# Stacking the position parts of latent scores, quartering the recurrence gates, and moving three products to the results' banks

## What is computed

```python
def mla_attention(c_q, c_kv, k_r, ...):          # S = 512, 8 heads, NOPE 64, ROPE 32
    q = (rms_norm(c_q, q_norm_g) @ w_uq).reshape(B, S, 8, 96)
    q_nope, q_rope = q[..., :64], apply_rope(q[..., 64:], cos, sin)
    kv = (rms_norm(c_kv, kv_norm_g) @ w_ukv).reshape(B, S, 8, 128)
    k_nope, v = kv[..., :64], kv[..., 64:]
    k_rope = apply_rope(k_r, cos, sin)           # one for all heads
    s = (einsum('bqhd,bkhd->bhqk', q_nope, k_nope) + einsum('bqhr,bkr->bhqk', q_rope, k_rope)) * scale
    return einsum('bhqk,bkhd->bqhd', softmax(s), v)

def rg_lru(x, wa, ba, wx, bx, lam):              # 16 blocks of 64 x 64, x is the convolved branch
    r  = sigmoid(einsum('bshi,hij->bshj', xb, wa) + ba)
    ig = sigmoid(einsum('bshi,hij->bshj', xb, wx) + bx)
    log_a = -8 * r * softplus(-lam)
    h = scan(exp(log_a), sqrt(-expm1(2 * log_a)) * (ig * x))
```

## Time and profile before

| | |
|---|---|
| median of three runs | 2161.89 us (2161.06 to 2163.26) |
| profiled execution, its own time | 2162.84 us |
| profiled execution, span | 2161.0 us |
| TensorE busy | 2124.9 us (98% of the span) |
| VectorE busy | 1136.9 us (53%) |
| ScalarE busy | 765.7 us (35%) |
| mean granted clock of TensorE | 0.997 |

### The profile page before, as it was taken

How to read it: one execution, slowest core, us unless ns; L and a number is a source line. 1 busy time by engine, 2 the same in 40 slices (tenths; PEclk the granted TensorE clock), 3 DMA queues, 4 the chain that set the end, 5 groups by cost and what they waited for, 6 DMA issues and landing times.

```text
span 2161.0 us, 28431 instructions
## 1 busy us (share of the span) xinstructions
PE 2124.9 (98%) x11767; PEld 1754.6 (81%) x11767; DVE 1136.9 (53%) x1535; ACT 765.7 (35%) x1224; POOL 123.6 (6%) x110
## 2 busy tenths in 40 slices
PE   8999999999999999999999999999999999999998
PEld 6888988678888887788888887787788887888887
DVE  5655557645655557654444445775653446333333
ACT  4251424532242425543222224353643234222222
POOL 0111100200011100200000003000000002000000
PEclk9999999999999999999999999999999999999999
DMA  6313222113313122113333224234022332332321
GB/s 186 99 59 116 80 59 81 40 40 109 100 47 118 60 70 70 40 59 97 97 97 97 98 98 127 79 117 136 21 78 98 98 98 88 96 98 91 100 95 65
DMA packets 158097, 189.04 MB, mean 87 GB/s; under 512 B 4194, under 2 KB 147876, under 8 KB 157860
## 3 DMA queue, kind: packets, MB, share of 16 engines
q1 hardware_dynamic: 153204, 174.41, 25.6%
q0 software_dynamic: 4608, 13.00, 1.9%
q10 hardware_dynamic: 176, 0.07, 0.0%
HBM read 182.20 MB, written 7.36 MB: 88 GB/s over the span
## 4 chain that ended last, share of the span: by engine, by line
PE 91%; DVE 5%; ACT 2%; POOL 1%; issue 1%; DMA 0%; POOLq 0%; DVEq 0%; ACTq 0%
PE PS L963 25%; PE PS L965 25%; PE PS L964 25%; PE PS L1085 5%; PE PS L1126 3%; PE PS L1097 3%; POOL X L930 1%; PE PS L971 1%; PE PS L975 1%; PE PS L972 1%; PE PS L1239 1%; PE PS L1044 0%; DVE WL L1941 0%; DVE UL L1994 0%; DVE TMP L2279 0%
## 5 line engine op out<-in xcount | busy, mean ns | idle before, releaser
L963 PE MATMUL PS<-UH,WH 128*128 128x512 f32 x1632 | 642.7, 394 | 7.5 <-DVE WL L2351 4.7
L965 PE MATMUL PS<-UH,WL 128*128 128x512 f32 x1632 | 637.0, 390 | 0.0
L964 PE MATMUL PS<-UL,WH 128*128 128x512 f32 x1632 | 636.4, 390 | 0.0
L1482 ACT ACTIVATE WH<-WS 128x2048 fp32r<-128x2048 f32 x98 | 187.9, 1918 | 618.1 <-PE PS L965 602.5
L963 PEld LDWEIGHTS PS<-UH,WH 128*128 128x128 f32 x1632 | 307.2, 188 | 75.4 <-DVE UL L1994 6.0
L965 PEld LDWEIGHTS PS<-UH,WL 128*128 128x128 f32 x1632 | 306.9, 188 | 64.7
L964 PEld LDWEIGHTS PS<-UL,WH 128*128 128x128 f32 x1632 | 307.3, 188 | 62.9 <-issue 0.7
L1941 DVE TENSOR_TENSOR WL<-WS,WH 128x2048 fp32r<-128x2048 f32 x98 | 224.4, 2290 | 229.9 <-ACT WH L1482 229.8
L2211 DVE TENSOR_TENSOR WL<-WS,WH 128x2048 fp32r<-128x2048 f32 x44 | 100.7, 2288 | 151.2 <-ACT WH L1636 151.2
L1636 ACT ACTIVATE WH<-WS 128x2048 fp32r<-128x2048 f32 x44 | 84.4, 1917 | 248.9 <-PE PS L965 246.7
L963 PE MATMUL PS<-WH,UH 128*128 128x256 f32 x416 | 118.6, 285 | 0.9 <-DVE PT L2310 0.9
(11 more groups left out here) (312 smaller groups left out, 3090.9 us busy)
## 6 DMA issues: line engine op xcount, KB each, us to landing
WS<-in_ffn_w SPq DMA_DIRECT2D x66, 1024.0 KB, 5.2
WS<-in_w_in SPq DMA_DIRECT2D x61, 1024.0 KB, 5.3
WS<-in_w_out SPq DMA_DIRECT2D x8, 1024.0 KB, 5.1
WS<-in_w_gate SPq DMA_DIRECT2D x8, 1024.0 KB, 5.5
WS<-in_w_attn_out SPq DMA_DIRECT2D x4, 1024.0 KB, 5.1
WS<-in_w_lru_out SPq DMA_DIRECT2D x4, 1024.0 KB, 5.2
WS<-in_w_o SPq DMA_DIRECT2D x4, 1024.0 KB, 5.1
bias_skewed<-bias_rows POOLq DMA_DIRECT2D x1, 3072.0 KB, 13.4
```

The source lines that it names most:

```text
L963: nc.tensor.matmul(dst, sh, mh, start=start, stop=False, skip_group_check=True)
L964: nc.tensor.matmul(dst, sh, ml, start=False, stop=False, skip_group_check=True)
L965: return nc.tensor.matmul(dst, sl, mh, start=False, stop=stop, skip_group_check=True)
L1482: nc.scalar.activation(WH[:, c % 2, 0:kt * n], staged(c, kt * n), ACT.Copy).then_inc(w_hi, 1)
```

## The change

It has eight parts.

1. *Position parts stacked.* The query tiles `QRH`, `QRL` and key tiles `KRH`, `KRL` give way to `QRS` and `KRS`, where high, high and low of a head's queries stand on 96 partitions against high, low and high of the keys. One product of 96 rows per head takes the place of three of 32. ScalarE fills two quarters of a head's stack (`stack_high`), VectorE the third (`stack_low`), heads 0 and 1 ahead of the items and heads 2 to 7 after items 0, 1, 2, 3, 6 and 7 of a layer. `QRH` now lies over `SQ`.
2. *Latent attention's start.* Scores wait for the first half of the low keys only; the second half is made after the first maxima. `expanded_values(1)` goes to pair 3. The table of the exponential is loaded ahead of the queries.
3. *Latent norms.* The second sum and the spread stand between the steps of `("ga", 1)`. All norms inside a product spread one step earlier.
4. *Products in pair 3.* `("v", 1)` of the dilated attention and `("xg", 3)` go to pair 3 as well.
5. *Gates on quarters.* A gate product becomes two of 64 x 64 weights; those of the second gate write the other half of the partitions, and ScalarE reads them across. `RGW` loses its zeros and the memset ahead of its load. Two buffers `XC`; `gated` runs one round later.
6. *Start.* `input_turned(1)` comes ahead of the first product, and the next two one round earlier; the product of the bias table moves behind the second dilated group.
7. *Order of a weight chunk.* `c0 + 3` is rounded earlier in the second layer, and later on VectorE in the first.
8. *POOL.* Its first transfers change places.

```diff
-                if (w, g, hh) == ("v", 0, 0):
+                if (w, g, hh) == ("v", 0, 0) or (w, g) == ("v", 1):
                     pl.aside((w, L, hh, g), "a", 3)
...
-                     lambda: pl.aside(("uv", L, 1), "a", 2))
+                     lambda: pl.aside(("uv", L, 1), "a", 3))
...
+    pl.aside(("xg", 3), "d", 3)
+    pl.add_chunk(("xg", 3), KD, CW, ("xg", 3))
...
-                for q, k in ((QRH, KRH), (QRH, KRL), (QRL, KRH)):
-                    for b in range(2):
-                        rows = slice((2 * j + b) % 4 * ROPE, (2 * j + b) % 4 * ROPE + ROPE)
-                        got.append((b, 0, S, q[rows, j // 2, tok], k[rows, :], False))
+                for b in range(2):
+                    got.append((b, 0, S, QRS[0:3 * ROPE, (2 * j + b) % 4, tok], KRS[0:3 * ROPE, :], False))
...
+        def heads_to_stack(name, n):
+            i = n - pl.item_at[name][0]
+            return {0: 2, 1: 3, 2: 4, 3: 5, 6: 6, 7: 7}.get(i)
...
                 if k == 5:
                     norm_sum(name, KD)
-                if k == 7:
+                if k == 6:
                     norm_spread(name)
...
                     for w in range(2):
-                        last = nc.tensor.matmul(pair(key)[:, w, :], RGW[:, w, 2 * j + m, :], XC[:, m, :],
-                                                start=True, stop=True)
+                        for b in range(2):
+                            last = nc.tensor.matmul(pair(key)[rows_of(b if w == 0 else 1 - b), w, :],
+                                                    RGW[rows_of(b), w, 2 * j + m, :], XC[rows_of(b), j % 2, m, :],
+                                                    start=True, stop=True, skip_group_check=True)
...
             input_turned(0)
             idle_products(9, bank(3)[:, 0:P])
+            input_turned(1)
...
-                    if c == 0 and k < 6:
-                        input_turned(1 + k // 2)
+                    if c == 0 and k < 4:
+                        input_turned(2 + k // 2)
...
-                norm_sum(("cq", L), QT)
-                norm_sum(("ckv", L), KT_KV)
-
-                def spread_c():
-                    norm_spread(("cq", L))
-                    norm_spread(("ckv", L))
-
-                feature_major(("ga", L, 1), between=spread_c)
+                def latent_norms(k):
+                    if k == 0:
+                        norm_sum(("cq", L), QT)
+                    if k == 1:
+                        norm_sum(("ckv", L), KT_KV)
+                    if k == 3:
+                        norm_spread(("cq", L))
+                        norm_spread(("ckv", L))
+
+                feature_major(("ga", L, 1), between=latent_norms)
...
-                pe.wait_ge(dve_out, pl.dve_out["uk", L, 1])
+                pe.wait_ge(dve_out, pl.dve_out["uk", L, 0])
                 pe.wait_ge(krope_lo, L + 1)
-                pe.wait_ge(qrope_lo, L + 1)
...
+            def stack_high(name, h):
+                if h >= 4:
+                    act.wait_ge(acc_ready, place_free(name, h))
+                for i in range(2):
+                    ins = nc.scalar.activation(QRS[quarter(i), h % 4, :],
+                                               QRH[quarter(h % 4), h // 4, :].bitcast(F32), ACT.Copy)
+                ins.then_inc(stack_hi, 1)
...
+            def stack_low(name, h):
+                if h >= 4:
+                    dve.wait_ge(acc_ready, place_free(name, h))
+                nc.vector.scalar_tensor_tensor(out=QRS[quarter(2), h % 4, :], in0=TMP[quarter(h % 4), h // 4, :],
+                                               scalar=MLA_SCALE, in1=QRH[quarter(h % 4), h // 4, :].bitcast(F32),
+                                               op0=ALU.mult, op1=ALU.subtract).then_inc(stack_lo, 1)
...
-                        if hh == 1 or i > (L == 0):
+                        if hh == 0 and i == 0:
+                            lo_of_chunk(c0 + 3)
+                        if hh == 1 or i > 1:
                             lo_of_chunk(pl.chunk[key] + 2)
...
-                if j > 0:
-                    dve.wait_ge(acc_ready, pl.acc["rg", 2 * j - 1])
-                    dve.wait_ge(gate_v, 2 * j)
+                if j > 1:
+                    dve.wait_ge(acc_ready, pl.acc["rg", 2 * j - 3])
+                    dve.wait_ge(gate_v, 2 * j - 2)
```

More of the change, by code:

```diff
@@ L441, in build_program @@
                               for i, name in enumerate(("QNH", "QNL", "KNH", "KNL")))
[L442 to L445, removed]
+        KRS = place("KRS", [P, S], F32R, offset=arena_at + 4 * 8192)
+        QRS = place("QRS", [P, 4, S], F32R, offset=arena_at + 4 * 15360)
         VM = view(6144, NT, S)
@@ L991, in feature_major @@
                         norm_between(norm, k)
-                    if between and k == 3:
-                        between()
+                    if between:
+                        between(k)
                     if new and new[0] == "cat":
@@ L1081, in scores @@
                     take_pair(("item", n))
+                    if kind == "mla" and it["first"]:
+                        pe.wait_ge(stack_hi, 8 * it["L"] + 2 * it["j"] + 2)
+                        pe.wait_ge(stack_lo, 8 * it["L"] + 2 * it["j"] + 2)
                     last = [None, None]
@@ L1283, in vectors_turned @@
                 last.then_inc(small_pe, 1)
-                pe.wait_ge(rel_in, 48)
-                nc.tensor.matmul(bank(6)[0:QH, 0:384], TBL, ONEHOT, start=True, stop=True).then_inc(small_pe, 1)
             input_turned(0)
             idle_products(9, bank(3)[:, 0:P])
+            input_turned(1)
             for k in range(0, KD, 2):
@@ L1321, in _ @@
                             continue
+                        if (w, L, hh, g) == ("k", 0, 0, 1):
+                            pe.wait_ge(small_dve, 2)
+                            pe.wait_ge(rel_in, 48)
+                            nc.tensor.matmul(bank(5)[0:QH, 0:384], TBL, ONEHOT, start=True, stop=True
+                                             ).then_inc(small_pe, 1)
                         if w == "v":
@@ L1424, in _, with last_queries @@
             pe.wait_ge(keys_in, 64)
-            attention(("swa",), lambda: feature_major(("wq", 3)))
+            def last_queries():
+                pe.wait_ge(dve_out, pl.dve_out["xg", 3])
+                feature_major(("wq", 3))
+            attention(("swa",), last_queries)
             for j in range(8):
@@ L1605, in attention @@
                 mla = name[0] == "mla"
-                table(ACT.Exp)
+                if not mla:
+                    table(ACT.Exp)
                 exp_of_item(n0)
@@ L1613, in attention @@
                     turned(n)
+                    if mla and heads_to_stack(name, n):
+                        stack_high(name, heads_to_stack(name, n))
                     if n > n0 and pl.items[n - 1]["last"] and not mla:
@@ L1759, in _ @@
                 act.wait_ge(krope_ready, L + 1)
[L1760 removed]
+                nc.scalar.activation(KRS[:, :], KRO[:, 0, :], ACT.Copy).then_inc(krope_hi, 1)
                 table(ACT.Sqrt)
@@ L1785, in _ @@
                                              ).then_inc(qrope_hi, 1)
+                        act.wait_ge(qrope_hi, L + 1)
+                        for h in range(2):
+                            stack_high(("mla", L), h)
                 def values_out(u):
@@ L2163, in attention @@
                     turned(n)
+                    if mla and heads_to_stack(name, n):
+                        stack_low(name, heads_to_stack(name, n))
                     if mla and it["last"]:
@@ L2437, in _, with low_keys @@
                 dve.wait_ge(qrope_hi, L + 1)
-                nc.vector.scalar_tensor_tensor(out=QRL[:, :, :], in0=TMP[:, :, :], scalar=MLA_SCALE,
-                                               in1=QRH[:, :, :].bitcast(F32), op0=ALU.mult, op1=ALU.subtract
-                                               ).then_inc(qrope_lo, 1)
-                for u in range(2):
+                for h in range(2):
+                    stack_low(("mla", L), h)
+                def low_keys(u):
                     key = ("uk", L, u)
@@ L2445, in _ @@
                        ).then_inc(dve_out, 1)
-                attention(("mla", L))
+                low_keys(0)
+                attention(("mla", L), lambda: low_keys(1))
                 for j in range(4):
```

90 lines of the change are left out of this document (58 added, 32 removed).

## The result

The changed kernel takes 2139.62 us (median of four runs, 2138.69 to 2140.05) against 2161.52 beside it on the same chip: ratio 0.9897, 95% interval 0.9886 to 0.9909. Forecast was 2127.0, range 2121 to 2139. The sign was right, 12.6 us of the gain are missing, and the time lies just outside the range.

A forecast was written before the change was run, and what follows sets the result against it. TensorE, busy 98% of the span, was taken to bound the kernel; terms from -11.5 (latent items) to +2.0 (stack waits) summed to -34.8 us, from 2162.8 to 2128.0, predicted as 2127 for the median, range 2121 to 2139.

The forecast's parts named there:

- the price of `stack_low`: Latent attention, VectorE: about 0.7 us per stack, taken to fit into its 1.96 us idle time in ordinary items.
- the stacks on the path: Latent attention: forecast +2.0 us (0 to +4); rival: TensorE waits 0.8 us in all twelve items, 9.4, total 2134.5, chance 0.12.
- The 2.0 us for items 3 and 7: Latent attention: stack ahead of the copy of the spread sums makes TensorE wait about 0.5 us twice a layer, +2.0 us.
- the item: Latent attention: stacked 96-row products save 0.36 us an item (0.30 to 0.40) over 32 items, -11.5 us.
- the gates: Gate products: sixteen pieces on array quarters, four at a time, -5.4 us; two at a time would give +1.6.
- the rival that row tiles cannot share a bank: Gates: one gate's two products go one after the other, 10.4 us more than forecast, total 2137.5; chance 0.12.
- the start: Program start: parts turned one round earlier end waits for rounded operands, small vectors and bias rows, -4.9 us (-3 to -5.5).
- `("v", 1)` and `("xg", 3)` in pair 3: Dilated attentions: scores' wait for the `("v", 1)` copy goes, -3.1 us; windowed attention: wait for `("xg", 3)` goes, -0.9 us.
- the chunk order: Second layer: TensorE's wait of 1.32 + 0.16 us for chunk `c0 + 3` goes, -1.5 us.
- the spreads: Mixing and second feed-forward parts: spreading norms one step earlier lets a normed product's first result leave sooner, -1.4 us.
- 2127 and 3.3: Rival: the clock falls nonetheless, or the start gives half, 3.3 us more, stated total 2130.5; chance 0.17.
- The clock term (-3.3): Behind the latent sums, both layers: clock no longer falls to half, saving 1.7 us each, -3.3 us (0 to -3.3).

The follow-up runs named there:

- the kernel with the chunks apart: Changed kernel with GpSimd's split of the output weight chunks begun after item 8 instead of item 0, its second chunk after item 11: 2124.84 us, ratio to before 0.9832.
- the kernel with two quarters: The kernel with the chunks apart, with the second gate's products kept on the first gate's quarters, so only two of four are used: 2131.57 us.
- part 1 alone: The kernel before with only the stacked position parts added, GpSimd's split where it was: 2168.47 us, ratio 1.0030.
- the sums together: The kernel with the chunks apart, with both latent sums together again ahead of the product ga 1, spread still one product earlier: 2127.82 us.

## Why the prediction was wrong, and where it was right

**The step that failed** is the price of `stack_low`. I put "0.7" us for each, from a neighbouring row, and asked only whether it fits into VectorE's gap. I did not ask what else uses what it uses. The price holds for twelve of the sixteen stacks; four, two in each layer, took 4.65 to 4.98 us. Each of the four made TensorE wait, 1.4 to 3.0 us, and three falls of the clock at 1.7 us came behind, which I had not priced either: 13.8 us in all by the stages. My bounds for the stacks on the path (0 to +4 us, rival 9.4) had no room for it, and no rival of mine named GpSimd, though the 12.85 us of its work stand in the very window that I used for VectorE's load.

**The sign was in my own rows.** The earlier trace rows has the copy of the spread sums with 2.11 us. I took that as its length. Of the eight such copies in the kernel before two took 2.11 and 2.12 us and six 0.43, and the summary of the line shows as much at a glance (nanoseconds, minimum, median, maximum):

```profile
L2089 DVE COPY ARENA<-RLM x8: 426/428/2122, 402.3 to 921.3; 128x512 f32<-128x512 f32 x8
```

The first long one began at 402.31, while GpSimd's subtraction ran from 399.56, in GpSimd's timeline of the kernel before:

```profile
399.56 4.57 POOL L895 TENSOR_TENSOR WL<-WS,WH 128x2048 fp32r<-128x2048 f32 x1
```

It ended 0.29 us after it. The rule is written down, too: the Trainium skill, "SBUF — State Buffer", section "Who interferes with whom", says that a VectorE instruction with two SBUF inputs, and a copy in a two-port mode, contends with a GpSimd instruction that reads SBUF, and that the one issued second blocks until the first is done. These traces agree: 4.67 and 4.98 us beside the subtraction, 1.97 and 2.31 beside casts, 2.37 to 2.40 for a cast behind a stack. With it the question would have been asked: two stacks a layer begin inside the 14 us of GpSimd's work.

**The 2.0 us for items 3 and 7** rested on the same 2.11 and were not needed: in the kernel with the chunks apart the copies behind items 3 and 7 take 0.43, and TensorE waits for none of the eight, not even for the two of 2.09. So the latent attention could give 13.3 + 2.0 us and the little that an item was better than forecast (0.37 for 0.36); the kernel with the chunks apart gets 15.7. The missing 11.4 us, these 2.0 and 0.4 are the 13.8 us by which after is longer there. The medians differ by 14.8; of the rest 0.6 stands ahead of the first scores, a stretch that differs as much between executions of kernels with the same start, and 0.3 at the last norm.

**Right, by the runs:** the item (12.1 us by undoing part 1), the gates with four quarters together (5.4 us; the rival that row tiles cannot share a bank is refuted for different partitions of a bank, the case here: the Trainium skill, "TensorEngine Tiling (Array Packing)", "Restrictions and Gotchas", has it so, and neither after nor the kernel with two quarters agrees). **Right by the trace alone**, not by a run of its own: the start (first `v` product at 37.93, forecast 38.4), `("v", 1)` and `("xg", 3)` in pair 3, the chunk order, the spreads. Two totals of rivals are up to 0.2 us off their own terms (12 waits of 0.8 are 9.6, not 9.4; 2127 and 3.3 are 2130.3, not 2130.5), which changes nothing.

**The clock term (-3.3)** was right for the profiled execution of the kernel before, which shows two falls, but it isn't fixed: 17 executions of that kernel gather at 2159.5 to 2160.2, 2161.2 to 2162.0 and 2163.0 to 2163.4, three groups some 1.6 apart, about the price of one fall (1.7). That they have two, one and no fall is argued: from the sizes, and from the mean granted clock on record, 0.997 in the upper group, 0.998 in the middle, 0.998 or 0.999 in the lower. Only one execution of it has a profile here. With part 1 alone the sums stand in the old order and no fall comes behind them in either layer. So that the profile had both falls was luck for this term.

## What to carry to other kernels

Before adding work to an engine's gaps, look at what runs on the others in the same microseconds: in these traces an instruction of VectorE with two inputs in SBUF, or a copy from SBUF to SBUF, that met one of GpSimd took what was left of the other's and then most of its own length. When a row's duration differs from its siblings' of the same shape, the difference is a cause to be named, not a length to be used. The cure was to let GpSimd begin later, or its work cut in pieces, and gave 14.5 to 14.8 us on top of the change's 22.

## What was not expected of the hardware

- VectorE and GpSimd block each other in both directions and by single instructions; the second to come runs on some 0.55 us past the end of the first (a 32x512 stack that takes 0.68 alone), or 0.29 us (the copy that takes 0.43 alone). The copies `PT` out of PSUM don't wait: the one at 388.38 takes 0.68 us beside a cast of GpSimd, as it does without.
- Four quarters of the array work at once, two of them into one bank and two into another: four starts within 0.02 us, 0.43 us to the next four.
- A fall of the clock can cost next to nothing: at 1758.67 after has one during the idle products ahead of the last norm, and the stage is 0.3 us longer, since TensorE would have waited 1.2 us behind them anyway (before has 1.02 of idle time at 1785.63, after none at 1762.98).
- Whether the clock falls behind the same order of work differs between the layers of one kernel (0.73 and 1.00 in the two windows with the sums together) and, as the mean clocks on record suggest, between executions of one kernel.
